# Prompt attention of a two-stream encoder layer: the weighted sum over keys put directly behind the next unit's transposes, and the addition of y put in front of the scans

## The reference, cut to what matters

```
z = einsum('bqhd,bkhd->bhqk', qb, kb) * scale
mask = kpos[None, :] < qpos[:, None]
log_one_minus = where(mask, log_sigmoid(-z), 0)
after = cumsum(log_one_minus, axis=3, reverse=True) - log_one_minus
a = where(mask, exp(log_sigmoid(z) + after), 0)
y_b[t] = sum_s a[t, s] * v[s]
```

## Time and profile before

| | before |
|---|---|
| median of 3 runs | 2316.68 us (2316.09 to 2316.88) |
| profiled execution, its own time | 2319.07 us |
| span of that profile | 2317.3 us |
| PE matmul busy | 2167.2 us (94%), 12884 instructions |
| DVE busy | 1317.6 us (57%) |
| POOL busy | 921.4 us (40%) |
| ACT busy | 746.1 us (32%) |
| mean granted TensorE clock | 0.973 of full |

### The profile page before, as it was taken

One profiled execution on the slowest core, in us unless ns is written; L12 is line 12 of the kernel. 1 busy time (PEld: TensorE's weight loads), 2 busy tenths in 40 slices (PEclk: granted clock), 3 DMA queues, 4 the chain that ended last, 5 costly groups with the idle time before them and its releaser, 6 DMA issues. The chain is left out here.

```text
span 2317.3 us, 33750 instructions
## 1 busy us (share of the span) xinstructions
PE 2167.2 (94%) x12884; PEld 2057.6 (89%) x12884; DVE 1317.6 (57%) x1715; ACT 746.1 (32%) x1435; POOL 921.4 (40%) x495
## 2 busy tenths in 40 slices
PE   6999999998898999989996989799999999999993
PEld 6999999998888999979996968799999999999992
DVE  5044120004777777856554557676776767667666
ACT  3222102225666766744332122212121121211212
POOL 2335334446655555547552210423324233242404
PEclk9999999999999999999997989899999999999996
DMA  5125324636544554565636342201111111111104
GB/s 171 46 78 178 119 76 135 170 125 164 147 113 111 140 131 122 136 186 145 183 105 197 112 163 87 87 28 55 39 43 48 34 54 36 45 45 36 45 0 165
DMA packets 290821, 237.40 MB, mean 102 GB/s; under 512 B 51142, under 2 KB 267926, under 8 KB 290710
## 3 DMA queue, kind: packets, MB, share of 16 engines
q1 hardware_dynamic: 281968, 222.24, 33.2%
q10 hardware_dynamic: 7510, 9.19, 1.3%
q0 software_dynamic: 1232, 4.46, 0.5%
HBM read 168.51 MB, written 67.33 MB: 102 GB/s over the span
## 5 line engine op out<-in xcount | busy, mean ns | idle before, releaser
L1131 DVE TENSOR_TENSOR_SCAN p_rest<-p_rest 128x896 f32<-128x896 f32 (+7 forms) x128 | 230.4, 1814 | 249.6 <-ACT p_rest L1064 249.2
L168 PE MATMUL p_psU<-mergedT_lo,p_w_hi 128*128 128x364 f32 x1056 | 347.0, 329 | 3.3 <-ACTq L2146 3.3
L170 PE MATMUL p_psU<-mergedT_hi,p_w_lo 128*128 128x364 f32 x1056 | 347.7, 329 | 0.0
L169 PE MATMUL p_psU<-mergedT_hi,p_w_hi 128*128 128x364 f32 x1056 | 347.3, 329 | 0.0
L148 POOL TENSOR_SCALAR p_w_hi<-p_w_raw 128x1024 fp32r<-128x1024 f32 x72 | 98.3, 1366 | 558.3 <-PE p_psD L170 417.4
L2169 DVE TENSOR_TENSOR p_acc<-p_psD,p_acc 128x512 f32<-128x512 f32 (+1 forms) x396 | 273.3, 691 | 45.3 <-PE p_psD L170 44.0
L282 PE MATMUL p_psB<-hT_lo,w_hi 128*128 128x364 f32 x888 | 295.6, 333 | 2.4 <-issue 2.4
L282 PE MATMUL p_psB<-hT_hi,w_lo 128*128 128x364 f32 x888 | 293.2, 330 | 0.0
L282 PE MATMUL p_psB<-hT_hi,w_hi 128*128 128x364 f32 x888 | 292.4, 329 | 0.0
L922 POOL TENSOR_TENSOR p_weights<-p_weights,p_rest 128x895 f32<-128x895 f32 (+7 forms) x128 | 171.1, 1348 | 184.2 <-DVE p_rest L1131 184.2
L168 PEld LDWEIGHTS p_psU<-mergedT_lo,p_w_hi 128*128 128x128 f32 x1056 | 199.2, 189 | 5.6 <-POOLq L132 3.4
(11 more groups left out here) (255 smaller groups left out, 4692.7 us busy)
## 6 DMA issues: line engine op xcount, KB each, us to landing
p_w_raw<-in_w_up SPq DMA_DIRECT2D x44, 512.0 KB, 3.7
w_raw<-in_w_in SPq DMA_DIRECT2D x40, 512.0 KB, 3.9
p_w_raw<-in_w_down SPq DMA_DIRECT2D x22, 512.0 KB, 3.5
p_kT<-k_hi_scratch SPq DMA_DIRECT2D x32, 256.0 KB, 4.7
p_kT<-k_lo_scratch SPq DMA_DIRECT2D x32, 256.0 KB, 5.2
w_raw<-in_w_gate SPq DMA_DIRECT2D x16, 512.0 KB, 4.0
p_raw_v<-in_cache_sb_v SPq DMA_DIRECT2D x8, 1024.0 KB, 6.1
p_raw_k<-in_cache_sb_k SPq DMA_DIRECT2D x7, 1024.0 KB, 6.4
```

What stands on the lines that cost most here:

```text
L168: nc.tensor.matmul(out, stat_hi, mov_lo, start=first, stop=False)
L169: nc.tensor.matmul(out, stat_hi, mov_hi, start=False, stop=False)
L170: return nc.tensor.matmul(out, stat_lo, mov_hi, start=False, stop=last)
L1131: nc.vector.tensor_tensor_scan(src, src, src, 1.0, ALU.mult, ALU.bypass).then_inc(s("scanned"), 1)
```

## The change

Three calls are moved inside the unit loops: on PE the weighted sum of the unit before goes directly behind the transposes, in front of filler and scores; on ACT and DVE the two steps that make y go in front of the sigmoids and scans. Nothing is added or removed, and the instruction lists of POOL and SP are the same.

```diff
@@ block.tensor
                 for k in range(len(UNITS)):
                     turn(k)
+                    if k:
+                        weighted_sum(k - 1)
                     pieces = [(b, part) for b in scored(k) for part in range(len(parts(tile_of(b))))]
...
                     fill(at + cuts[-2], cuts[-1] - cuts[-2])
-                    if k:
-                        weighted_sum(k - 1)
                 weighted_sum(len(UNITS) - 1)
@@ block.scalar
                     split_hi(k)
+                    if g == 0 and w:
+                        y_low_rows(w - 1)
                     for b in scored(k):
                         sigmoids(b)
                     for e in range(groups_ended(k), groups_ended(k + 1)):
                         empty(e)
-                    if g == 0 and w:
-                        y_low_rows(w - 1)
@@ block.vector
                     split_lo(k)
+                    if g == 0 and w:
+                        y_sum(w - 1)
                     for b in scored(k):
                         scan(b)
-                    if g == 0 and w:
-                        y_sum(w - 1)
```

## The result

The changed kernel takes 2352.95 us (median of 4 runs, 2349.9 to 2353.25) against 2316.78 us before (median of 4): 1.0154 times, 95% interval 1.0136 to 1.0171. The profiled execution spans 2351.2 us where the one before spans 2317.3 us, 33.9 us more.

The account below looks back on a forecast made before the run. PE was taken to bound the kernel late in the attention stage, with waits earlier; the terms summed to 43.9 us on the profiled 2319.07 us, 2363.0, less 2.4 us for the profile: forecast 2360 us, range 2344 to 2370 us.

Parts of the forecast that it names:

- The sum: All terms over the attention stage added: 28.1 + 11.9 + 3.4 + 1.7 - 1.2 = 43.9 us slower.
- Store heads, the wait for y: Starts of heads 1, 2 and 7 to 11: 3.07 us cover lost plus 0.95 us later scores; 7 x 4.0 = 28.1 us.
- The early store heads: Heads 1 and 2, where q's stores come besides: taken at the same 4.0 us each, plus 1.7 us each for the clock.
- the alternative: Heads 1 and 2, if the scores have slack there: 3.1 us each, 1.9 us less in all.
- The clock: Heads 1, 2 and 7 to 11: PE runs slower after each new 3.9 us wait; 7 x 1.7 = 11.9 us.
- Clean heads: Starts of heads 12 to 15: transposes of (3,0) wait 0.86 us each for tile 7's `weigh`, 3.4 us in all.
- Split heads: Starts of heads 3 to 6: the 2.92 us wait inside the transposes grows by 0.42 us each, 1.7 us in all.
- The end: At the stage's last weighted sum y is ready, so the 1.19 us wait goes: -1.2 us.
- The moved steps at nothing: ACT's and DVE's moved steps, 0.38 and 0.42 us, cost nothing because the scores they wait for come later by more.
- The correction left out: w_lo on POOL in heads 7 to 11, shorter while DVE stands still: 0.27 us each, 1.4 us back, outside the sum.

Follow-up runs that it names:

- a_store_first: Changed kernel with the store of y moved on SP to the head of each unit's list, ahead of the next weight block's load: 2323.76 us.
- a_keep31: Changed kernel, but in unit (3,1) alone the weighted sum of (3,0) stands behind filler and scores again: 2336.53 us.
- b_store_first: Kernel before the change, with the store of y moved on SP to the head of each unit's list: 2309.26 us.
- a_defer: a_store_first with every split of a filler block on POOL and its load on SP put off to the next unit (3,0): 2294.10 us.
- pe_only: Kernel before the change, with only PE's weighted sum moved behind the transposes, ACT and DVE as before: 2405.16 us.

## Why the prediction was right, and where it was off

**The sum.** The terms add up to 43.9 us, and the two profiled spans are 33.9 us apart. Of the 10 us, 7.4 are in the two early heads, 1.6 in the five store heads (5 x 5.7 = 28.5 forecast, 26.9 measured) and 1.5 in the split heads (1.7 forecast, 0.2 measured); what is left comes to about half a microsecond the other way. That the forecast was off by 7 us and not by 10 has nothing to do with the mechanism: the sum starts from the profiled execution before, which lay 2.4 us above its median, and the changed kernel's (2353.0 us) lay on its median. In the sum without the clock's term a slip of 0.1 us stands, 32.0 and not 31.9.

**Store heads, the wait for y.** Right in place and mechanism, shown by a_store_first and a_keep31. The term was 4.0 us for each of heads 7 to 11. Read in head 7: PE reached the sum at 771.75 + 0.69 = 772.44 and began at 776.26, 3.82 us (forecast 3.9). Before, it stood longer than the 0.72 us of the row: in b_store_first, where nothing ends the stretch early, the filler and scores of (3,1) run from 762.98 to the sum at 765.89, 2.91 us, so PE arrived at 767.24 + 2.91 = 770.15 and waited 0.88 us. The cover was 2.9 us and not 3.07. With 0.6 us at the transposes the head loses 3.82 - 0.88 + 0.6 = 3.5 us ahead of the clock. Of the 0.95 us by which the scores come later, 0.67 us arrive at y, which DVE makes 9.05 us behind the head's first transposes as against 8.38 us before.

**The early store heads.** This step failed: "In the two early heads POOL is busy without a break and I take the same value". Heads 1 and 2 gained 2.95 and 1.10 us where 4.0 and the clock's 1.7 us stood for each, 11.4 us in all. In head 1 y comes when it did before (594.35, and 594.32 in the changed kernel), whatever PE does, since the store in front of it leaves SP at 587.22 before and at 587.51 now and lands no later:

```profile
587.13 1.94 PE L1008 MATMUL p_psY<-p_aT,p_v 128*128 128x256 f32 x8 [1.77 <-DVE p_yb L1146]
...
594.32 0.42 DVE L1146 TENSOR_TENSOR p_yb<-p_psY,p_ytmp 64x256 f32<-64x256 f32 x1 [5.25 <-DMA yb_scratch<-p_yb]
...
594.88 1.19 PE L1008 MATMUL p_psY<-p_aT,p_v 128*128 128x256 f32 x8 [0.17 <-DVE p_yb L1146]
```

The sum starts at 594.88 as against 594.91 before. PE came late to it, held up by a wait for the y before and then by the lower clock, and both lay inside the time that it would have waited anyway. What was lost is the cover alone, 2.9 us; neither the 0.95 us nor the clock's price could be added. In head 2 not even the whole cover is lost anew: its first sum starts at 625.73 as against 624.18, 1.55 us later, though the head itself starts 3.3 us later, so that over both heads one cover and these 1.55 us are gone, 4.5 us where the table has 4.1 and head 0 its 0.3. I had written down 3.1 us each as the alternative and not taken it, but it would have mended only 1.9 of the 7.4 us.

**The clock.** The stretches came in each of heads 7 to 11. In a_store_first the same filler and scores of (3,1) in head 7 run at the full clock:

```profile
774.66 0.33 PE L282 MATMUL p_psD<-hT_hi,w_hi 128*128 128x364 f32 x1
...
777.47 0.49 PE L993 MATMUL p_psT<-ident,p_weights 128*128 128x128 f32 x3
```

That is 2.81 us, so the slow stretch cost 4.36 - 2.81 = 1.55 us in head 7. The same comparison of unit (3,1), less the wait at the sum, gives 1.5, 2.6, 1.5 and 1.3 us in heads 8 to 11, 8.5 us for the five, as the forecast had it (5 x 1.7). But the rule drawn from the rows was too neat. In the changed kernel a wait of 3.07 us at the start of head 3 brought no slow stretch:

```profile
649.79 0.44 PE L993 MATMUL p_psT<-ident,p_weights 128*128 128x128 f32 x2 [3.07 <-POOL p_weights L922]
...
651.39 0.33 PE L282 MATMUL p_psD<-hT_lo,w_hi 128*128 128x364 f32 x1
651.56 0.33 PE L282 MATMUL p_psD<-hT_hi,w_hi 128*128 128x364 f32 x1
```

Filler starts 0.17 us apart there, and head 3 is 0.94 us shorter than before for it. In b_store_first a wait of 2.94 us at the start of head 5 brought none either, and the head takes 28.69 us where it took 30.2 us before:

```profile
702.48 0.66 PE L993 MATMUL p_psT<-ident,p_weights 128*128 128x128 f32 x4 [2.94 <-POOL p_weights L922]
...
703.14 0.33 PE L282 MATMUL p_psD<-hT_hi,w_hi 128*128 128x364 f32 x1
703.31 0.33 PE L282 MATMUL p_psD<-hT_hi,w_lo 128*128 128x364 f32 x1
```

In a_keep31 waits of 1.4 us with shorter ones close behind brought one, twice. The Trainium skill ("TensorE: Matmul & The Clock Gate", HAM oscillation) describes a loop in which a wait in each round makes each round start slow; the five store heads agree, head 3 here and head 5 of b_store_first do not.

**Clean heads.** Forecast 0.86 us each, measured 0.69 to 0.84; a_defer shows the same in all heads. The profile names only 0.39 to 0.57 us of it as idle; by the starts of the transposes the wait is 0.55 to 0.74 us, see below.

**Split heads.** Forecast 0.42 us each, measured 0.35 to 0.41 in heads 4 to 6. In head 3 the clock stayed up and the head got shorter.

**The end.** The wait of 1.19 us at the last sum is gone from the list, as forecast.

**The moved steps at nothing.** Right for the whole change and for the reason given, but the reason carries more than I saw: pe_only shows that without the moves on ACT and DVE the y would have been late at every sum with g = 0. And DVE's own new lateness behind the store, costed at nothing, is about a microsecond in a_keep31, where nothing longer hides it.

**The correction left out.** Rightly so: w_lo took 2.65 us in head 7, as before, though DVE stood still for part of it. But the reading of the two rows as a stretching by a tenth was wrong. What counts is a scan that is running when w_lo starts. At the start of head 5 of the changed kernel w_lo took 4.22 us:

```profile
702.12 2.79 DVE L1131 TENSOR_TENSOR_SCAN p_rest<-p_rest 128x1024 f32<-128x1024 f32 x1 [1.71 <-ACT p_rest L1064]
702.86 4.22 POOL L151 TENSOR_TENSOR w_lo<-w_raw,w_hi 128x1024 fp32r<-128x1024 f32 x1
```

It ended 707.08 - 704.91 = 2.17 us behind the scan. So did every w_lo of the stage, before and changed, that started inside a scan, 2.15 to 2.21 us behind it, whether it took 2.64 or 4.22 us; those that started outside one took 2.36 to 2.43 us, also where a scan began later beside them. In head 7 the scan at the start of w_lo is there in both kernels, and DVE's standing still comes behind it, so there was nothing to give back. This agrees with the lock that the Trainium skill ("SBUF — State Buffer", two separate sides) describes: who comes second waits for a whole instruction. In the split heads of the changed kernel w_lo is 1.85 us longer by it and w_hi, which before stood inside the scan (3.03 us), is 1.97 us shorter, so that the split takes nearly as long as before, 5.3 and 5.4 us.

## What to carry to other kernels

Ask of every piece of work that stands in front of a waiting instruction what it covers: moving the waiter ahead costs the cover's whole length when what it waits for is timed by another queue, here 2.9 us in each store head and 1.3 to 2.6 us more for the clock. On SP the small store left 0.43 us behind the load in front of it and so as late as POOL's split let that load go; follow such a wait back to the DMA's issue and to what held the instruction ahead of it, before moving anything on the engines. Curing that queue's order and the place of POOL's long steps was worth 33 to 35 us; the early sum gained nothing in any pair of kernels that differ by it alone or with its two companions, and cost 11 us where nothing else was late.

## What the runs showed of the hardware

The idle time that a profile names before a matmul is too short by some 0.2 us, since the modelled end of the matmul ahead reaches into it. At the start of head 7 the two groups of four transposes start 767.64 - 766.65 = 0.99 us apart, against 0.41 us where nothing waits, 0.58 us of wait where the row says 0.40; at the sum behind it 3.82 us where the row says 3.58.

Length alone does not tell whether a wait is followed by a stretch at the lower clock: 3.07 us was not in one head of the changed kernel, and 3.06 to 3.08 us was in the heads after it; 2.94 us was not in head 5 of b_store_first; 1.4 us with shorter waits behind it was in two heads of a_keep31.

A GpSimd instruction that starts while a scan runs on VectorE ends a fixed time behind the scan: 2.15 to 2.21 us for w_lo, 0.84 to 0.86 us for w_hi, where they take 2.36 to 2.43 and 1.04 to 1.06 us on their own.
